# Moving two VectorE steps and one ScalarE step ahead of a weight split in a mixture-of-experts loop

## The chip, the cores and the metric

One core of a Trainium2 chip runs the whole layer as one program. The metric is the device time of one execution in microseconds; lower is better. Engines run their own instruction lists in order and wait for each other on semaphores: TensorE (PE) multiplies, ScalarE (ACT) and VectorE (DVE) do elementwise work, GpSimd (POOL) issues gathers and scatters, SyncE (SP) issues the loads of weights.

## The reference

A hybrid encoder layer over 1536 tokens of 1024 channels: two mixers (a gated spatial one and windowed attention), then a hierarchical mixture of experts. Only the last part matters here:

```python
def expert_block(args):
    xblk, e = args
    hid = jax.nn.silu(xblk @ w_gate[e]) * (xblk @ w_up[e])
    return hid @ w_down[e]

yb = lax.map(expert_block, (xb, block_e)).reshape(P, D)
y = jnp.zeros((T + 1, D), h.dtype).at[slot_tok].add(yb * slot_w[:, None])
```

Each token goes to two of 32 experts. The token rows of an expert are padded to blocks of 128. `w_gate` and `w_up` of an expert are 1024x512, `w_down` is 512x1024, all float32.

## The kernel before, in words

The mixers and the routing take the first two thirds of the time; then the expert loop runs over the blocks, one block of 128 rows in each trip, from trip 1 (written out once) through a hardware loop from 2 to `m`, with a short prologue and an epilogue.

**Split products.** Each float32 product is made of three matmuls over rounded parts: hi by hi, hi by lo and lo by hi. ScalarE makes the hi part by a rounding copy, and VectorE makes the lo part, the raw value less hi. This holds for the weights (`split_hi`, `split_lo`, in halves 0 and 1 of 128x2048 numbers, for g = gate, u = up, d = down), for the turned input rows (`x_hi`, `x_lo`, L2071 and L2142, two pieces each) and for the turned hidden rows (`hidden_hi`, `hidden_lo`, L2086 and L2157).

**TensorE in trip i** (`tensor`): `gate_up(i)` (gate product of block i into one PSUM bank, then its up product into another, 48 matmuls), `turn_x(i + 1)` (eight transposes of the gathered rows of the next block, L1984), `down(i - 1)` (24 matmuls), `turn_hidden(i)` (four transposes of `hid`, L2018). The first matmul of `gate_up` is on L1994, the first of `down` on L2008. `turn_hidden(i)` waits for `hid` of block i; `gate_up(i + 1)` waits for `x_lo(i + 1)` and, half by half, for the lo weights; `down(i)` waits for `hidden_lo(i)`. In trip 1 the order differs: `down(0)` lies between the gate and the up product, so that `turn_x(2)` is followed at once by `turn_hidden(1)`. The epilogue runs `gate_up(m + 1, "g")`, `down(m)`, `gate_up(m + 1, "u")`.

**ScalarE in body(i)** does, in order: g half 0 of the next block, `tanh(i)` (L2076), g half 1, u half 0, `x_hi(i + 1)`, u half 1, d half 0, `weigh(i - 1)` (scales the result rows, L2082), d half 1, `hidden_hi(i)`. **VectorE in body(i)**: g half 0, `glu_gate(i)` (L2148), g half 1, u half 0, `glu_up(i)` (L2153, which writes `hid`), `x_lo(i + 1)`, u half 1, d half 0, d half 1, `hidden_lo(i)`. A split of weights of half h waits until the data has landed and until TensorE has used the old half (`used`), and `split_lo` waits for its `split_hi`. `glu_up(i)` waits for `used["u"]` of both halves, the end of the up product.

**Loads.** Each weight has one raw buffer (`held_wg`, `held_wu`, `held_wd`), in two halves of 1 MB. The SyncE list issues the load of the block after next (of the next block for d) in the order g0, g1, u0, u1, d0, d1, each once VectorE has finished the split of that half (`lo_done`). A load is left out where the block has the same expert as the one before. GpSimd gathers the rows of block i + 2 after `turn_x(i + 1)` has read the buffer, and scatters block i - 1 after `weigh(i - 1)`; the next `weigh` waits until that scatter has landed (a copy into `e_prv` on POOL comes in between).

Of the kernel before, what the change touches and what calls it, by code (L numbers as in the profile page):

```python
# [1892 lines left out]
def experts(nc, a, held):  # L1893
# [34 lines left out]
    def half(t, h):  # L1928

        k = t.shape[1] // 2  # L1930
        return t[:, h * k:(h + 1) * k, :]

    def first(i):
        return isinstance(i, int) and i == 0


    def blocks(eng):

        eng.wait_ge(tab_in, 2 * 16)
        return eng.value_load(tab[0:1, 2 * TW + 2:2 * TW + 3], min_val=2 * T // P - 3, max_val=MAXB - 3)  # L1940
# [115 lines left out]
    def scalar(act):  # L2056
        def split_hi(i, w, h):

            act.wait_ge(w_in[w][h], (i + 2) * 16)
            if not first(i):  # L2060
                act.wait_ge(used[w], i * 2 + (h - 1))
            elif w == "g":
                act.wait_ge(s_up_ps, 1)
            else:
                act.wait_ge(s_up_ps if w == "u" else s_down_ps, 2)
            act.activation(half(hi[w], h), half(raw[w], h), ACT.Copy).then_inc(hi_done[w], 1)  # L2066

        def x_hi(i):
            for b in range(2):
                act.wait_ge(x_ps, i * 2 + (b + 5))  # L2070
                act.activation(half(xT_hi, b), ps_x[b][:].rearrange("p (k q) -> p k q", k=4),  # L2071
                               ACT.Copy).then_inc(x_hi_done, 1)

        def tanh(i):
            act.wait_ge(used["g"], i * 2 + 2)
            act.activation(th, ps_g[:], ACT.Tanh, scale=0.5).then_inc(tanh_done, 1)  # L2076

        def weigh(i):
            act.wait_ge(used["d"], i * 2 + 2)
            act.wait_ge(shifted, i + 1)  # L2080
            for h in range(2):
                act.activation(yo[:, h * 512:(h + 1) * 512], ps_y[h][:], ACT.Copy, scale=prv[:, 1:2]).then_inc(yo_done, 1)  # L2082

        def hidden_hi(i):
            act.wait_ge(h_ps, i + 3)
            act.activation(hidT_hi, ps_h[:].rearrange("p (k q) -> p k q", k=DE // P), ACT.Copy).then_inc(hid_hi_done, 1)  # L2086

        def body(i):
            split_hi(i + 1, "g", 0)
            tanh(i)  # L2090
            split_hi(i + 1, "g", 1)
            split_hi(i + 1, "u", 0)
            x_hi(i + 1)
            split_hi(i + 1, "u", 1)
            split_hi(i, "d", 0)
            weigh(i - 1)
            split_hi(i, "d", 1)
            hidden_hi(i)

        chosen_act = held["chosen_act"]  # L2100
        split_hi(0, "g", 0)
        split_hi(0, "g", 1)
        chosen_act["tanh"](act, 1)
        chosen_act["turned_hidden"](act, 0)
        split_hi(0, "u", 0)
        split_hi(0, "u", 1)
        chosen_act["turned_hidden"](act, 1)
        chosen_act["weigh"](act, 0)
        x_hi(0)
        split_hi(0, "d", 0)  # L2110
        split_hi(1, "g", 0)
        chosen_act["weigh"](act, 1)
        tanh(0)
        split_hi(1, "g", 1)
        split_hi(0, "d", 1)
        x_hi(1)
        hidden_hi(0)
        split_hi(1, "u", 0)
        split_hi(1, "u", 1)
        body(1)  # L2120
        m = blocks(act)
        with act.Fori(2, m + 1) as i:
            body(i)
        tanh(m + 1)
        split_hi(m + 1, "d", 0)
        split_hi(m + 1, "d", 1)
        weigh(m)
        hidden_hi(m + 1)
        weigh(m + 1)

    def vector(dve):
        dve.sem_inc(lo_done["d"], 2)

        def split_lo(i, w, h):

            dve.wait_ge(hi_done[w], i * 2 + (h + 1))
            dve.tensor_tensor(half(lo[w], h), half(raw[w], h), half(hi[w], h).bitcast(F32), ALU.subtract).then_inc(lo_done[w], 1)  # L2137

        def x_lo(i):
            for b in range(2):  # L2140
                dve.wait_ge(x_hi_done, i * 2 + (b + 5))
                dve.tensor_tensor(half(xT_lo, b), ps_x[b][:].rearrange("p (k q) -> p k q", k=4),  # L2142
                                  half(xT_hi, b).bitcast(F32), ALU.subtract).then_inc(x_lo_done, 1)

        def glu_gate(i):

            dve.wait_ge(tanh_done, i + 3)
            dve.scalar_tensor_tensor(out=th, in0=th, scalar=1.0, in1=ps_g[:], op0=ALU.add, op1=ALU.mult).then_inc(glu_done, 1)  # L2148

        def glu_up(i):  # L2150
            dve.wait_ge(glu_done, i + 3)
            dve.wait_ge(used["u"], i * 2 + 2)
            dve.scalar_tensor_tensor(out=hid, in0=th, scalar=0.5, in1=ps_u[:], op0=ALU.mult, op1=ALU.mult).then_inc(hid_done, 1)  # L2153

        def hidden_lo(i):
            dve.wait_ge(hid_hi_done, i + 3)
            dve.tensor_tensor(hidT_lo, ps_h[:].rearrange("p (k q) -> p k q", k=DE // P), hidT_hi.bitcast(F32),  # L2157
                              ALU.subtract).then_inc(hid_lo_done, 1)

        def body(i):  # L2160
            split_lo(i + 1, "g", 0)
            glu_gate(i)
            split_lo(i + 1, "g", 1)
            split_lo(i + 1, "u", 0)
            glu_up(i)
            x_lo(i + 1)
            split_lo(i + 1, "u", 1)
            split_lo(i, "d", 0)
            split_lo(i, "d", 1)
            hidden_lo(i)  # L2170

        split_lo(0, "g", 0)
        split_lo(0, "g", 1)
        held["chosen_dve"]["glu"](dve, 1)
        split_lo(0, "u", 0)
        split_lo(0, "u", 1)
        x_lo(0)
        split_lo(0, "d", 0)
        split_lo(1, "g", 0)
        glu_gate(0)  # L2180
        split_lo(1, "g", 1)
        glu_up(0)
        x_lo(1)
        split_lo(0, "d", 1)
        hidden_lo(0)
        split_lo(1, "u", 0)
        split_lo(1, "u", 1)
        body(1)
        m = blocks(dve)
        with dve.Fori(2, m + 1) as i:  # L2190
            body(i)
        glu_gate(m + 1)
        split_lo(m + 1, "d", 0)
        split_lo(m + 1, "d", 1)
        glu_up(m + 1)
        hidden_lo(m + 1)
# [194 lines left out]
```

## Time and profile before

| What | us |
|---|---|
| median of three executions | 2113.71 (2113.36 to 2115.78) |
| the profiled execution, its time | 2113.9 |
| the profiled execution, its span | 2112.1 |
| PE busy / DVE busy / ACT busy | 2086.8 / 1278.4 / 1072.8 |
| granted clock of TensorE, mean | 0.997 of full speed |

The span is the time between the first and the last instruction that the trace has; the execution's own time is 1.8 us longer. PE is marked busy nearly all the time, but that average says little of single waits: they are read from the list of waits and from the timeline. A "window" row gives, for a stretch of time, the busy time of each engine in it and the mean busy share of the 16 DMA engines (a share can come out a little over 1).

### The profile page before, as it was taken

The numbers are of one execution on the slowest core, as the hardware profiler recorded it, in microseconds if no ns is written. First come the engines' busy times: TensorE is split into PE (matmuls) and PEld (weight loads), VectorE is DVE, ScalarE is ACT, GpSimd is POOL, SyncE is SP. The second block draws the span as 40 slices with busy tenths as digits, with TensorE's granted clock in tenths as the row PEclk, the third lists the DMA queues.
The fourth block names the chain that finished last, engine by engine and source line by source line (L and its number), as shares of the span: only waits on it lengthen the run. The fifth ranks groups of instructions, "written<-read, shape, count | busy, mean of one in ns | idle before, by whom it ended". The sixth has DMA issues, their size and how long they took to land.

```text
span 2112.1 us, 30313 instructions
## 1 busy us (share of the span) xinstructions
PE 2086.8 (99%) x10284; PEld 1733.2 (82%) x10284; DVE 1278.4 (61%) x1651; ACT 1072.8 (51%) x1584; POOL 467.8 (22%) x653
## 2 busy tenths in 40 slices
PE   8999999999999999999999999999999999999997
PEld 7788888888788888897888888757888888888886
DVE  5664233465554233565553424369999999998995
ACT  4553333344542432345533332138888888887884
POOL 4251011210451011203510012002222222122321
PEclk9999999999999999999999999999999999999999
DMA  7312322443113322552123224487998689999892
GB/s 226 101 41 90 97 84 92 137 181 99 62 52 114 100 90 80 174 170 75 41 80 95 86 80 168 176 347 276 362 383 319 235 313 335 384 376 370 289 343 64
DMA packets 108658, 379.46 MB, mean 180 GB/s; under 512 B 13506, under 2 KB 19827, under 8 KB 82964
## 3 DMA queue, kind: packets, MB, share of 16 engines
q1 hardware_dynamic: 91812, 335.64, 43.9%
q0 software_dynamic: 16752, 42.56, 7.5%
q8 instruction: 59, 0.97, 0.2%
q14 instruction: 35, 0.29, 0.0%
HBM read 402.78 MB, written 34.60 MB: 207 GB/s over the span
## 4 chain that ended last, share of the span: by engine, by line
PE 50%; DMA 4%; DVE 1%; ACT 1%; issue 1%; POOL 0%; POOLq 0%; SPq 0%; ACTq 0%; DVEq 0%
PE main L532 3%; PE main L534 3%; PE main L533 3%; DMA held_wu<-w_up_e 3%; PE main L2008 3%; PE main L2010 3%; PE main L2009 3%; PE main L1996 3%; PE aux L1994 3%; PE main L1994 3%; PE main L1995 3%; PE aux L1996 3%; PE aux L1995 3%; PE main L520 2%; PE main L522 2%; PE main L521 2%
## 5 line engine op out<-in xcount | busy, mean ns | idle before, releaser
L984 DVE TENSOR_TENSOR w_lo<-raw,w_hi 128x1024 fp32r<-128x1024 f32 (+1 forms) x216 | 250.4, 1180 | 316.7 <-ACT w_hi L728 316.6
L728 ACT ACTIVATE w_hi<-raw 128x1024 fp32r<-128x1024 f32 (+1 forms) x216 | 211.5, 1005 | 143.4 <-PE main L534 73.9
L532 PE MATMUL main<-e_g_hi,w_hi 128*128 128x512 f32 x576 | 237.4, 412 | 0.0
L534 PE MATMUL main<-e_g_hi,w_lo 128*128 128x512 f32 x576 | 225.7, 392 | 0.0
L533 PE MATMUL main<-e_g_lo,w_hi 128*128 128x512 f32 x576 | 225.0, 391 | 0.0
L2137 DVE TENSOR_TENSOR e_d_lo<-held_wd,e_d_hi 128x2048 fp32r<-128x2048 f32 x76 | 173.8, 2289 | 52.1 <-ACT e_d_hi L2066 51.9
L520 PE MATMUL main<-w_hi,e_g_hi 128*128 128x512 f32 (+1 forms) x560 | 203.7, 364 | 1.2 <-DVE e_g_lo L998 0.6
L522 PE MATMUL main<-w_hi,e_g_lo 128*128 128x512 f32 (+1 forms) x560 | 200.1, 357 | 0.0
L521 PE MATMUL main<-w_lo,e_g_hi 128*128 128x512 f32 (+1 forms) x560 | 199.9, 357 | 0.0
L2137 DVE TENSOR_TENSOR e_u_lo<-held_wu,e_u_hi 128x2048 fp32r<-128x2048 f32 x76 | 173.4, 2284 | 14.0 <-ACT e_u_hi L2066 14.0
L2137 DVE TENSOR_TENSOR e_g_lo<-held_wg,e_g_hi 128x2048 fp32r<-128x2048 f32 x76 | 173.6, 2284 | 3.7 <-ACT e_g_hi L2066 3.7
L2066 ACT ACTIVATE e_u_hi<-held_wu 128x2048 fp32r<-128x2048 f32 x76 | 145.7, 1920 | 31.2 <-PE main L1996 15.9
L2066 ACT ACTIVATE e_d_hi<-held_wd 128x2048 fp32r<-128x2048 f32 x76 | 145.8, 1918 | 21.4 <-PE main L2010 11.5
L2066 ACT ACTIVATE e_g_hi<-held_wg 128x2048 fp32r<-128x2048 f32 x76 | 145.9, 1919 | 14.8 <-DMA held_wg<-w_gate_e 13.8
L534 PEld LDWEIGHTS main<-e_g_hi,w_lo 128*128 128x128 f32 x576 | 108.4, 188 | 23.3
L533 PEld LDWEIGHTS main<-e_g_lo,w_hi 128*128 128x128 f32 x576 | 109.1, 189 | 19.1
L532 PEld LDWEIGHTS main<-e_g_hi,w_hi 128*128 128x128 f32 x576 | 109.0, 189 | 18.8
L1994 PE MATMUL aux<-e_g_hi,e_xT_hi 128*128 128x512 f32 x304 | 122.2, 402 | 0.6 <-DVE e_xT_lo L2142 0.5
L2008 PE MATMUL main<-e_d_hi,e_hidT_hi 128*128 128x512 f32 x304 | 121.6, 400 | 0.7 <-DVE e_hidT_lo L2157 0.7
L819 ACT ACTIVATE pr<-sm,stat,rsq 128x384 f32<-128x384 f32 (+1 forms) x96 | 64.5, 671 | 111.7 <-DVE stat L1251 105.7
L520 PEld LDWEIGHTS main<-w_hi,e_g_hi 128*128 128x128 f32 x560 | 106.5, 190 | 16.2 <-DVE e_g_lo L998 1.0
L522 PEld LDWEIGHTS main<-w_hi,e_g_lo 128*128 128x128 f32 x560 | 106.4, 190 | 15.2
(360 smaller groups left out, 4704.4 us busy)
## 6 DMA issues: line engine op xcount, KB each, us to landing
held_wg<-w_gate_e SPq DMA_DIRECT2D x78, 1024.0 KB
held_wu<-w_up_e SPq DMA_DIRECT2D x78, 1024.0 KB
held_wd<-w_down_e SPq DMA_DIRECT2D x76, 1024.0 KB
raw<-w_in SPq DMA_DIRECT2D x120, 512.0 KB, 3.6
raw<-w_proj_b SPq DMA_DIRECT2D x24, 512.0 KB, 3.6
raw<-w_proj_a SPq DMA_DIRECT2D x24, 512.0 KB, 3.7
raw<-w_out SPq DMA_DIRECT2D x24, 512.0 KB, 4.1
raw<-w_in SPq DMA_DIRECT2D x24, 256.0 KB, 4.5
```

Source lines behind the costliest of these rows:

```text
L520: pe.matmul(bank[:, 0:n], stat_hi(k), hi[:, k, 0:n], start=(k == 0), stop=False)
L521: pe.matmul(bank[:, 0:n], stat_hi(k), lo[:, k, 0:n], start=False, stop=False)
L522: mm = pe.matmul(bank[:, 0:n], stat_lo(k), hi[:, k, 0:n], start=False, stop=(k == KT - 1))
L532: pe.matmul(bank[:], hi[:, k, :], mov_hi[:, k, :], start=(k == 0), stop=False)
L533: pe.matmul(bank[:], hi[:, k, :], mov_lo[:, k, :], start=False, stop=False)
L534: mm = pe.matmul(bank[:], lo[:, k, :], mov_hi[:, k, :], start=False, stop=(k == KT - 1))
L728: act.activation(hi, buf, ACT.Copy).then_inc(w_hi_done, 1)
L984: dve.tensor_tensor(lo, buf, hi.bitcast(F32), ALU.subtract).then_inc(w_split, 1)
L1994: pe.matmul(ps[:], xT_hi[:, k, :], hi[w][:, k, :], start=(k == 0), stop=False)
L2008: pe.matmul(ps_y[h][:], hidT_hi[:, k, :], hi["d"][:, k, c], start=(k == 0), stop=False)
L2066: act.activation(half(hi[w], h), half(raw[w], h), ACT.Copy).then_inc(hi_done[w], 1)
L2137: dve.tensor_tensor(half(lo[w], h), half(raw[w], h), half(hi[w], h).bitcast(F32), ALU.subtract).then_inc(lo_done[w], 1)
```

## The change

In ScalarE's body, `x_hi(i + 1)` now comes before the split of u half 0 and no longer after it. In VectorE's body, `glu_up(i)` and `x_lo(i + 1)` come before the split of u half 0 and no longer after it. Nothing is added or taken away; the prologue, the epilogue and the lists of the other engines are the same.

```diff
@@ scalar, body(i)
             split_hi(i + 1, "g", 1)
+            x_hi(i + 1)
             split_hi(i + 1, "u", 0)
-            x_hi(i + 1)
             split_hi(i + 1, "u", 1)
@@ vector, body(i)
             split_lo(i + 1, "g", 1)
-            split_lo(i + 1, "u", 0)
             glu_up(i)
             x_lo(i + 1)
+            split_lo(i + 1, "u", 0)
             split_lo(i + 1, "u", 1)
```

## Rows read from the trace of the kernel before

**Rows 1.** The page: span and number of instructions

```profile
span 2112.1 us, 30313 instructions
```

**Rows 2.** Waits of PE, expert loop (who for whom: us, times, longest)

```profile
PE aux L2018 <- DVE e_hid L2153: 2.6, 4, 1.4
...
PE aux L1994 <- DVE e_xT_lo L2142: 0.5, 1, 0.5
```

**Rows 3.** One of 35 windows of one block's length each

```profile
1843.37:1861.13 17.76, 17.76 (x87) 14.90 (x86) 16.29 (x12) 14.50 (x12) 3.42 (x4) 1.00 1.01 391
```

**Rows 4.** Timeline, trip 1 (start, length, engine, line, tiles, idle before)

```profile
1448.69 2.29 DVE L2137 TENSOR_TENSOR e_u_lo<-held_wu,e_u_hi 128x2048 fp32r<-128x2048 f32 x1 [3.19 <-ACT e_u_hi L2066]
...
1448.97 0.40 PE L1996 MATMUL main<-e_u_hi,e_xT_lo 128*128 128x512 f32 x1
...
1449.85 1.08 ACT L2071 ACTIVATE e_xT_hi<-aux 128x512 fp32r<-128x512 f32 x2 [1.20 <-PE aux L1984]
...
1450.89 0.68 DVE L2153 SCALAR_TENSOR_TENSOR e_hid<-e_th,main 128x512 f32<-128x512 f32 x1
...
1451.63 0.75 PE L2018 MATMUL aux<-ident,e_hid 128*128 128x128 f32 x4 [1.37 <-DVE e_hid L2153]
...
1452.91 0.47 PE L1994 MATMUL aux<-e_g_hi,e_xT_hi 128*128 128x512 f32 x1 [0.53 <-DVE e_xT_lo L2142]
```

**Rows 5.** The chain that ended last, prologue (start, length, what)

```profile
1431.37 0.61 ACT e_xT_hi L2071
1432.00 0.70 DVE e_xT_lo L2142
```

**Rows 6.** Timelines of ACT and DVE, one block in the middle

```profile
1727.82 1.92 ACT L2066 ACTIVATE e_u_hi<-held_wu 128x2048 fp32r<-128x2048 f32 x1 [0.38 <-PE main L1996]
1730.93 1.09 ACT L2071 ACTIVATE e_xT_hi<-aux 128x512 fp32r<-128x512 f32 x2 [1.19 <-PE aux L1984]
1731.90 1.92 ACT L2066 ACTIVATE e_u_hi<-held_wu 128x2048 fp32r<-128x2048 f32 x1
...
1730.00 2.28 DVE L2137 TENSOR_TENSOR e_u_lo<-held_wu,e_u_hi 128x2048 fp32r<-128x2048 f32 x1
1732.20 0.68 DVE L2153 SCALAR_TENSOR_TENSOR e_hid<-e_th,main 128x512 f32<-128x512 f32 x1
```

**Rows 7.** Timeline of SP's queue, the same block (issues of two halves each)

```profile
1727.63 2.90 SPq L1890 DMA_DIRECT2D held_wg<-w_gate_e  x2
1732.63 4.08 SPq L1890 DMA_DIRECT2D held_wu<-w_up_e  x2
```

**Rows 8.** Timelines of ACT and PE, end of a long stretch of loads

```profile
1945.88 1.92 ACT L2066 ACTIVATE e_u_hi<-held_wu 128x2048 fp32r<-128x2048 f32 x1 [2.71 <-DMA held_wu<-w_up_e]
...
1960.37 1.92 ACT L2066 ACTIVATE e_g_hi<-held_wg 128x2048 fp32r<-128x2048 f32 x1 [1.02 <-DMA held_wg<-w_gate_e]
1964.21 1.92 ACT L2066 ACTIVATE e_u_hi<-held_wu 128x2048 fp32r<-128x2048 f32 x1 [1.91 <-DMA held_wu<-w_up_e]
...
1932.01 0.64 PE L2018 MATMUL aux<-ident,e_hid 128*128 128x128 f32 x4
...
1950.77 0.75 PE L2018 MATMUL aux<-ident,e_hid 128*128 128x128 f32 x4 [0.84 <-DVE e_hid L2153]
...
1969.10 0.75 PE L2018 MATMUL aux<-ident,e_hid 128*128 128x128 f32 x4 [0.17 <-DVE e_hid L2153]
```

**Rows 9.** Timelines of ACT, DVE and PE, last trip and epilogue

```profile
2070.19 1.09 ACT L2071 ACTIVATE e_xT_hi<-aux 128x512 fp32r<-128x512 f32 x2 [1.19 <-PE aux L1984]
...
2081.42 0.68 DVE L2157 TENSOR_TENSOR e_hidT_lo<-aux,e_hidT_hi 128x512 fp32r<-128x512 f32 x1
...
2082.34 0.49 PE L2008 MATMUL main<-e_d_hi,e_hidT_hi 128*128 128x512 f32 x1 [0.32 <-DVE e_hidT_lo L2157]
```

**Rows 10.** Timeline of POOL, one block in the middle

```profile
1712.37 2.20 POOL L2232 COPY e_prv<-held_slots 128x2 f32 x1 [7.27 <-DMA y<-e_yo,e_prv]
...
1714.52 0.17 POOL L2205 COPY e_nxt<-held_slots 128x2 f32 x1
```

## The prediction, made before the changed kernel was run

> **What bounds the kernel now.** I read the page first, for the span of 2112.1 us [rows 1], then the expert loop, where the diff lies, in windows of one block each. A window of 17.76 us has PE busy for all 17.76, DVE for 16.29 and ACT for 14.50 [rows 3]; so do nearly all of the 35. PE sets the pace of the loop, and an order of the splits can give time only where PE waits for DVE or ACT. The DMA share is the second thing to see there: 20 of the 35 windows stand at 0.99 or more, in runs of 6, 2, 10 and 2 blocks. In those the loads take all the bandwidth there is, and a block's loads take longer than PE's 17.76 us: u half 0 landed 18.33 us apart (1945.88 and 1964.21) [rows 8]. PE stays ahead only by the slack that the raw buffers hold.
>
> Third, the list of PE's waits, from the start of the loop to the end of the program: four waits for `hid`, 2.6 us in all with 1.4 the longest, and one of 0.5 for `x_lo` [rows 2]. That is nearly all that the change can take away. The timeline says where they are. In trip 1, `glu_up(1)` could have run from the end of the up product at 1449.37 (1448.97 + 0.40), but DVE was in the split of u0 from 1448.69 and it started at 1450.89; PE's transposes of `hid` came at 1451.63 and the next gate product at 1452.91 [rows 4]. Two more are at the end of the run of ten saturated blocks. From 1932.01 PE's transposes of `hid` came at 1950.77 and 1969.10, which is 18.76 and 18.33 and not 17.76 apart, so 1.00 and 0.57 us lost [rows 8]. There DVE and ACT wait for u0 to land, with `glu_up` queued behind. The fourth is in the epilogue, which stays as it is.
>
> **Part 1: trip 1.** The moved steps keep their durations. `x_hi` starts at 1449.85, since its transposes release it [rows 4], not the split before it; on DVE `glu_up` starts at about 1449.4, takes 0.68 and ends near 1450.1, before PE is through with its transposes. PE then waits only for the first piece of `x_lo`. DVE starts that 0.63 us after ACT started on its piece, and takes 0.70 [rows 5]; PE follows 0.05 behind, as it does after `hid` (1450.89 + 0.68 to 1451.63, 0.06) [rows 4]. So the gate product starts at 1449.85 + 0.63 + 0.70 + 0.05 = 1451.23 and not at 1452.91: **1.68 us gained**. Bounds: nothing, if some other input of PE is late, and 2.2, if PE had no wait at all there. I take 1.68; it rests on measured steps.
>
> What is late next: u0's hi starts 0.97 after `x_hi` (1730.93 to 1731.90), its lo 1.92 + 0.03 later, then DVE's splits start 2.20 apart (1730.00 to 1732.20) [rows 6]. Lo of u0 ends at 1449.85 + 0.97 + 1.95 + 2.28 = 1455.05; PE asks for it after 24 of 72 matmuls, a third of a period without its transposes, so about 5.5 us after 1451.23: 1456.7. It is covered by 1.6 us. `hidden_lo(1)` starts 2.92 + 4 x 2.20 = 11.72 after `x_hi` and ends 1462.3; `down(1)` asks at about 1463.0. If these covers went, the 1.68 would shrink by the shortfall.
>
> **Part 2: a block in the middle.** ACT did u0 from 1727.82 and then waited 1.19 us for `x_hi`'s transposes, at 1730.93. Now it stands idle until 1730.93 and u0 starts at 1731.90 [rows 6], 4.08 later. DVE starts u0's lo at 1731.90 + 1.95 = 1733.85 and not at 1730.00: 3.85 later; by then it has done `glu_up` and `x_lo` (0.68 and twice 0.70), which come earlier by about 1.7 and 1.2. Through u1, d0, d1 the delay melts, for DVE used to stand idle 1.47 us of a block (17.76 less 16.29 [rows 3]), all of it ahead of d1: u1 and d0 are 2.1 later, d1, `hidden_lo` and the next g0 0.5 later. DVE's work stays 16.3 of 17.76 us, so the delay doesn't grow from trip to trip. The nearest asker, `down`, wants `hidden_lo` over 5 us after it is done. Here the move costs **0**, hidden behind PE's matmuls; what it costs without that cover is the 3.85.
>
> **Part 3: the loads.** No load is moved on SP, but each waits for its lo split, so u0's is issued 3.85 later (1732.63 becomes 1736.5) and d0 behind it 2.1; g0 goes from 1727.63 to 1728.1 [rows 7]. A half takes 18.33 / 6 = 3.06 us when the loads are saturated [rows 8]. At the start of a saturated run, the queue holds g0 and g1 only, 6.1 us of work, and u0 comes 8.4 us behind: the DMA engines stand still for up to 2.3 us once, and by the u0 issue the whole run is late by at most 1736.5 - 2 x 3.06 - 1727.63 = 2.7 us. Afterwards six halves fill 18.3 us of a 17.76 us block, so the queue isn't dry again. Bounds: 0 (loads were queued already) and 2.7; I take 2.7.
>
> **Part 4: the end of the long run.** Now `hid` stands behind g1's split, not u0's. g1's hi began on its landing at 1960.37, 3.84 us before u0's [rows 8]. With all 2.7 us of lag: 1963.07, lo at 1965.02, `glu_up` 1967.22, `hid` with PE at 1967.96, against an unstalled 1932.01 + 2 x 17.76 = 1967.53. The first piece of `x_lo`, 0.60 behind `glu_up` and 0.75 long with its hand-over, is ready at 1968.57, 0.5 after PE wants it. So 0.5 us of the 1.57 stays: **1.07 gained**, bounds 0 and 1.57. u0, landed at 1966.9, has its lo by 1971.4, before PE's up product at 1973.5.
>
> **Part 5: the epilogue.** `down(m)` comes early there, behind one gate product. `hidden_lo(m)` started 11.23 after `x_hi` (2070.19 to 2081.42) and PE was already waiting for it: it began `down` at 2082.34 [rows 9]. By the new order it starts 11.72 after `x_hi`: **0.5 us lost**, between 0 and 0.6.
>
> **Sum**: -1.68 - 1.07 + 0.5 = -2.25 us. The profiled execution took 2113.9, its span 2112.1 [rows 1] and 1.8 around it; the span should become 2109.9, and that execution's time 2111.65. The median of the runs was 0.2 lower, so 2111.4.
>
> **GpSimd** shares the change too. A copy of two numbers into `e_prv` took 2.20 us while DVE was in a split, the same kind of copy 0.17 right after it [rows 10]. DVE now has its four splits u0, u1, d0, d1 in one piece around the time of the scatter, which can hold the scatter back by about one split, 2.2 us. The next scaling of rows waits for that scatter, and POOL's gather stands behind it in line; the next scaling comes after PE's `down`, whose end the transposes of `hid` mark at 1932.01 - 12 x 17.76 = 1718.89 [rows 8], and the copy ended at 1714.57, so there are over 4 us. So it costs nothing in the sum, and 2.2 us at most a block where that cover is gone. The Trainium skill, SBUF — State Buffer, "SBUF: two separate sides", says that a VectorE instruction with two SBUF inputs holds a port pair that GpSimd shares, so the other blocks for the whole instruction; by that rule the price is one split for each operation of GpSimd that meets one, and the sum stays at -2.25 as long as the 4 us hold. The trace agrees: that 2.20 us copy ended with the split.
>
> **The rivals.** (a) *Nothing arrives.* The wait in trip 1 turns into one for another input, such as the rest of `x_lo`, and the lag of the loads eats all of part 4. Only the epilogue's 0.5 is left: 2114.2. For it: DVE has 1.5 us to spare in a block. Against it: each hand-over in part 1 is measured. (b) *The loads run dry again and again*, which is the slower side. If the 2.3 us of standstill of part 3 came in every block of the run of ten and not once, PE would end it some 20 us later: about 2132. It decides from the point where six halves take less than PE's 17.76 us, or where the queue empties before u0's issue; with 3.06 us a half it keeps 0.6 us more work each block than PE takes, and the share near 1.0 in all ten windows speaks against it. (c) *More is gained than the profiled execution shows.* The three executions differ by 2.4 us, and such a difference can come from the saturated runs; one that lost 4 us there could win them all. 2109. (d) The scatter of the GpSimd rule comes too late in all 36 trips of the loop: 2113.7 + 36 x 0.3 = 2124 if it overran by 0.3 us a block.
>
> **How the numbers follow.** Forecast -2.25 us: 0.76. (a) 0.11, (b) 0.05, (c) 0.06, (d) 0.02. A measurement of this kernel tells a difference of 0.2% from none, which is 4.2 us: under 2109.5 is faster, over 2117.9 slower. The likeliest case and (a) are both inside; so faster 0.06, within 0.2% 0.87, slower 0.07. The likeliest case with its bounds (gain of 1.68 + 1.57 without loss; only part 1 less the epilogue) runs from 2110.5 to 2112.5. With the scatter of three executions and (a), I give 2109.8 to 2115.0.
>
> **What would show it.** In the list of PE's waits, the 1.4 us for `hid` in trip 1 is gone and the gate product of trip 2 begins some 1.4 us after the first transposes of x are out. In a block in the middle, ACT is idle some 3.6 us ahead of `x_hi`, and u0's lo starts 2.9 us after `x_hi`. The period stays 17.76. SP's u loads come 3.85 later, the DMA share stays about 1.0 in the same windows, and PE loses at most 0.5 us at the end of the run of ten. `down` in the epilogue starts 0.5 us later in relation to the last `x_hi`. The prediction is wrong if the period of an ordinary block grows, if u0 or u1 become what PE waits for, or if the loads lag by clearly more than 2.7 us.

## The result and the profile after

The change made the kernel slower: 2143.18 us, median of four executions (2137.20 to 2147.26), against 2113.53 (2113.24 to 2115.78) for the kernel before, a ratio of 1.0131 with a 95% interval of 1.0117 to 1.0145. The ratio is the estimate on record with its interval; the two medians by themselves give 1.0140. I had forecast 2111.4 and nothing measurable. The profiled execution has a span of 2135.4 us, 23.3 more than before [rows 1]; at 2137.20 it was the quickest of the four, so its rows show the loss at its smallest.

First, the list of PE's waits in the expert loop and behind it, of the changed kernel:

```profile
PE aux L1984 <- DMA e_xg<-h2s,e_nxt: 24.8, 19, 2.1
PE main L2008 <- DVE e_hidT_lo L2157: 1.2, 2, 0.8
PE aux L2018 <- DVE e_hid L2153: 1.1, 2, 0.9
PE aux L1994 <- DVE e_xT_lo L2142: 0.4, 1, 0.4
```

The four waits for `hid` of 2.6 us in [rows 2] have become two of 1.1. A new line stands above them: nineteen times the transposes of the next block's rows waited until the gathered rows `e_xg` had landed. Nothing of that kind was in the kernel before. The 24.8 us are the loss of this execution, and a little of it was won back.

Next, what was meant to happen. The timeline of trip 1 of the changed kernel, TensorE, VectorE and ScalarE:

```profile
1445.34 0.40 PE L1996 MATMUL main<-e_u_hi,e_xT_lo 128*128 128x512 f32 x1
...
1446.59 0.75 PE L2018 MATMUL aux<-ident,e_hid 128*128 128x128 f32 x4
1447.77 0.47 PE L1994 MATMUL aux<-e_g_hi,e_xT_hi 128*128 128x512 f32 x1 [0.43 <-DVE e_xT_lo L2142]
...
1445.84 0.69 DVE L2153 SCALAR_TENSOR_TENSOR e_hid<-e_th,main 128x512 f32<-128x512 f32 x1 [3.99 <-PE main L1996]
1446.84 1.29 DVE L2142 TENSOR_TENSOR e_xT_lo<-aux,e_xT_hi 128x512 fp32r<-128x512 f32 x2 [0.31 <-ACT e_xT_hi L2071]
...
1446.21 1.09 ACT L2071 ACTIVATE e_xT_hi<-aux 128x512 fp32r<-128x512 f32 x2 [8.30 <-PE aux L1984]
```

From the end of the up product to the next gate product PE needs 2.03 us (1445.74 to 1447.77), where it needed 3.54 before [rows 4]. Part 1 was right: 1.51 us against the 1.68 forecast.

The middle of the loop, VectorE and SP's queue in a trip before the long run of loads, still of the changed kernel:

```profile
1788.66 0.68 DVE L2153 SCALAR_TENSOR_TENSOR e_hid<-e_th,main 128x512 f32<-128x512 f32 x1
1789.71 1.29 DVE L2142 TENSOR_TENSOR e_xT_lo<-aux,e_xT_hi 128x512 fp32r<-128x512 f32 x2 [0.38 <-ACT e_xT_hi L2071]
1792.01 4.49 DVE L2137 TENSOR_TENSOR e_u_lo<-held_wu,e_u_hi 128x2048 fp32r<-128x2048 f32 x2 [1.00 <-ACT e_u_hi L2066]
1796.42 4.49 DVE L2137 TENSOR_TENSOR e_d_lo<-held_wd,e_d_hi 128x2048 fp32r<-128x2048 f32 x2
...
1786.29 3.15 SPq L1890 DMA_DIRECT2D held_wg<-w_gate_e  x2
1794.64 2.55 SPq L1890 DMA_DIRECT2D held_wu<-w_up_e  x2
```

VectorE has the schedule of part 2: a pause of 1.00 us ahead of u0, then u0, u1, d0, d1 without a gap, 8.9 us long (the x2 rows are two splits each). The up load follows the gate load by 8.35 us, as worked out (8.4), where it was 5.0 before [rows 7].

Now the engine that I had costed at nothing. GpSimd's timeline, one turn in the long run of loads, of the changed kernel:

```profile
1870.64 1.00 POOL L2232 COPY e_prv<-held_slots 128x2 f32 x1 [10.62 <-DMA y<-e_yo,e_prv]
1871.59 2.26 POOL L2205 COPY e_nxt<-held_slots 128x2 f32 x1
1874.72 2.21 POOL L2208 DMA_INDIRECT e_xg<-h2s,e_nxt  x1 [0.87 <-ACT e_yo L2082]
1877.24 2.44 POOL L2212 DMA_INDIRECT y<-e_yo,e_prv  x1 [0.31 <-issue]
1889.99 0.76 POOL L2232 COPY e_prv<-held_slots 128x2 f32 x1 [10.32 <-DMA y<-e_yo,e_prv]
```

and one turn of the kernel before, in its run of ten saturated blocks:

```profile
1856.01 0.64 POOL L2232 COPY e_prv<-held_slots 128x2 f32 x1 [8.82 <-DMA y<-e_yo,e_prv]
1856.59 0.18 POOL L2205 COPY e_nxt<-held_slots 128x2 f32 x1
1857.64 1.05 POOL L2208 DMA_INDIRECT e_xg<-h2s,e_nxt  x1 [0.87 <-POOL e_nxt L2205]
1863.34 1.59 POOL L2212 DMA_INDIRECT y<-e_yo,e_prv  x1 [4.65 <-ACT e_yo L2082]
1874.04 0.37 POOL L2232 COPY e_prv<-held_slots 128x2 f32 x1 [9.10 <-DMA y<-e_yo,e_prv]
```

GpSimd's list is a ring: a scatter must land before `e_prv` is copied, then comes `e_nxt`, the next gather, and the next scatter. From start to start the hops are:

| hop, us | before | after |
|---|---|---|
| copy of `e_prv` to copy of `e_nxt` | 0.58 | 0.95 |
| copy of `e_nxt` to gather | 1.05 | 3.13 |
| gather to scatter, less the wait for `e_yo` | 5.70 - 4.65 = 1.05 | 2.52 |
| scatter, its landing, to copy of `e_prv` | 10.70 | 12.75 |
| the ring without that wait | 13.38 | 19.35 |

Some 0.3 us of the third hop after the change is idle time at issue that the wait covered before. VectorE in the same turn of the changed kernel:

```profile
1869.31 4.49 DVE L2137 TENSOR_TENSOR e_u_lo<-held_wu,e_u_hi 128x2048 fp32r<-128x2048 f32 x2 [1.00 <-ACT e_u_hi L2066]
1873.72 4.49 DVE L2137 TENSOR_TENSOR e_d_lo<-held_wd,e_d_hi 128x2048 fp32r<-128x2048 f32 x2
```

All four of GpSimd's operations start inside these splits. The copy of `e_prv` ends at 1871.64 and that of `e_nxt` at 1873.85, with the first and the second split (1871.60 and 1873.80); the gather and the scatter end at 1876.93 and 1879.68, which is not the end of a split.

Before, the ring had 4.65 us to spare. After, it has nothing to spare and is longer than PE's 17.76 us. The gather stands in this ring, so the whole loop turns at the ring's pace: in the nineteen blocks with a wait, PE's transposes of `hid` are 18.95 to 20.12 us apart. The windows of two blocks of the changed kernel, against [rows 3]:

```profile
1852.47:1872.11 19.64, 18.03 (x85) 14.82 (x84) 16.37 (x12) 14.13 (x13) 7.85 (x5) 1.00 0.99 355
1872.11:1891.22 19.11, 18.03 (x85) 14.82 (x84) 16.39 (x12) 14.14 (x13) 7.62 (x5) 1.00 1.00 363
```

PE is busy 18.03 of 19.64 and of 19.11 us, at the same granted clock of 1.00, and POOL is busy 7.85 and 7.62 us a block where it was 3.42. That last number points to the cause: GpSimd has the same work to do and is busy for more than twice as long.

### The profile page after: what moved, and what is told of

The parts are those of the page before. It is cut to its first block, busy times and chain, and to the rows that moved or that the text cites. A ratio compares the mean times of both kernels' runs of the same rounds, so it can differ in the third digit from the quotient of the medians.

```text
span 2135.4 us, 30313 instructions
## 1 busy us (share of the span) xinstructions
PE 2087.1 (98%) x10284; PEld 1728.6 (81%) x10284; DVE 1279.6 (60%) x1651; ACT 1060.7 (50%) x1584; POOL 571.6 (27%) x653
## 4 chain that ended last, share of the span: by engine, by line
PE 69%; DMA 16%; issue 6%; POOL 3%; ACT 2%; DVE 2%; POOLq 0%; ACTq 0%; DVEq 0%
DMA y<-e_yo,e_prv 11%; PE main L534 10%; PE main L532 10%; PE main L533 10%; PE main L520 6%; PE main L522 6%; PE main L521 6%; PE aux L566 2%; DMA e_xg<-h2s,e_nxt 2%; POOL e_nxt L2205 2%; PE aux L585 1%; PE main L585 1%; PE main L2008 1%; PE main L2010 1%; PE main L2009 1%
## 5 line engine op out<-in xcount | busy, mean ns | idle before, releaser
L2066 ACT ACTIVATE e_u_hi<-held_wu 128x2048 fp32r<-128x2048 f32 x76 | 141.4, 1917 | 0.0
L533 PEld LDWEIGHTS main<-e_g_lo,w_hi 128*128 128x128 f32 x576 | 109.1, 189 | 19.1
L2232 POOL COPY e_prv<-held_slots 128x2 f32 x36 | 35.7, 991 | 325.5 <-DMA y<-e_yo,e_prv 322.4
L2010 PE MATMUL main<-e_d_hi,e_hidT_lo 128*128 128x512 f32 x304 | 118.8, 391 | 0.0
```

What stands on the lines that cost most here:

```text
L533: pe.matmul(bank[:], hi[:, k, :], mov_lo[:, k, :], start=False, stop=False)
L2010: mm = pe.matmul(ps_y[h][:], hidT_lo[:, k, :], hi["d"][:, k, c], start=False, stop=(k == DE // P - 1))
```

## Experiments

The case before the first runs: theory A, the ring on GpSimd sets the pace; theory B, the later loads leave the DMA engines idle (rival b of the prediction, whose 2132 was the nearest of my numbers to the result). B came near the size, but had not the wait that the trace shows. The code below is shortened.

### GpSimd's gather ahead of the landing

```diff
@@ gpsimd, loop of the changed kernel
+            pool.wait_ge(x_ps, i * 2 + 8)
+            pool.wait_ge(x_in, i * 16 + 64)
+            gather(i + 2, i + 3)
             pool.wait_ge(y_out, i * 16 + 16)
             pool.tensor_copy(prv, entry(i - 1)).then_inc(shifted, 1)
-            pool.wait_ge(x_ps, i * 2 + 8)
-            pool.wait_ge(x_in, i * 16 + 64)
-            gather(i + 2, i + 3)
```

> The changed kernel, with one more move, on GpSimd alone: in each trip the gather of the rows of block i + 2 goes ahead of the wait for the landed scatter and of the copy into e_prv. Theory A (GpSimd's ring: scatter, landing, copy, copy, gather, scatter takes some 19.3 us against a period of 17.76, and the gathered rows come too late for the transposes): the gather no longer stands behind the landing, PE's wait for e_xg (24.8 us in 19 waits) goes, and the time falls to 2111 to 2114. Theory B (the later loads leave the DMA engines idle; rival b of the prediction): nothing about the loads is changed, so the time stays near 2140, and PE waits for the lo weights or hid once the rows are there.

Measured: 2118.49 us, 1.0014 of before (1.0003 to 1.0026). The waits for `e_xg` are gone, and most of the loss with them. PE's waits in that kernel:

```profile
PE main L2008 <- DVE e_hidT_lo L2157: 9.5, 10, 3.3
PE aux L1994 <- DVE e_xT_lo L2142: 0.6, 2, 0.4
PE aux L2018 <- DVE e_hid L2153: 0.2, 1, 0.2
```

The rule by which the loads are issued was not touched, which speaks against B. It does not yet rule B out: in the long run of loads the up load follows the gate load by 6.8 us in this kernel, where the changed one has over 9. And 9.5 us of waits ahead of `down` are new (the profiled execution was the slowest of the ten, at 2124.01), and the time is above my 2111 to 2114. Some cost came with this edit or stayed from the change.

### Each engine's part alone

```diff
@@ vector, body (run: VectorE alone)
-            split_lo(i + 1, "u", 0)
             glu_up(i)
             x_lo(i + 1)
+            split_lo(i + 1, "u", 0)
@@ scalar, body (run: ScalarE alone)
+            x_hi(i + 1)
             split_hi(i + 1, "u", 0)
-            x_hi(i + 1)
@@ vector, body (run: glu_up alone)
+            glu_up(i)
             split_lo(i + 1, "u", 0)
-            glu_up(i)
             x_lo(i + 1)
```

> The kernel before with VectorE's part of the change alone: glu_up and x_lo ahead of the split of u half 0, ScalarE in the old order. Theory A: the four splits u0, u1, d0, d1 of VectorE follow each other without a break, as in the changed kernel, so GpSimd's copies, gathers and scatters run into them and the time is slow too, 2125 to 2145, with PE waiting for e_xg. Theory B: the u loads are issued 2.8 us later and not 3.85, so less is lost: 2114 to 2128, and PE's waits are for weights.

Measured: 2131.73 us, 1.0070 (1.0047 to 1.0094). PE waited 16.8 us in 17 waits for `e_xg`. VectorE's half alone brings the wait on the gathered rows, as A says. The time is inside A's range of 2125 to 2145 and above B's of 2114 to 2128, and the kind of wait is A's.

> The kernel before with ScalarE's part of the change alone: x_hi ahead of the split of u half 0, VectorE in the old order. By the schedule of the rows, VectorE does u0's lo at x_hi + 2.92, glu_up at + 5.12, x_lo at + 5.72, and PE can start the gate product at + 6.47; with 11.65 us from there to the next x_hi the period is some 18.1 us, so 36 trips lose 0.36 us each: 2125 to 2128, PE waiting for hid and x_lo. Theory A expects no wait for e_xg here, since x_lo still parts the splits of u0 and u1. Theory B, with the same late u loads as in the changed kernel, expects at least the changed kernel's loss in the saturated windows: 2140 or more.

Measured: 2138.16 us, 1.0105 (1.0082 to 1.0128), and not one wait for `e_xg`. The line that speaks is PE's weight loads, in small waits at 37 of the 38 blocks:

```profile
PEld aux L2018 <- DVE e_hid L2153: 24.7, 37, 5.6
```

The period is 18.13 us in most blocks, as worked out (18.1). The 0.37 us above 17.76 make 13 us over 36 trips. I had left out trips 1 and 2 and the epilogue, which lost 3.8, 2.2 and 3.8 us more. The time is far above the 2125 to 2128 that I gave, and close to B's 2140; but the loss is not where B has it. The up loads follow the gate loads by 6.9 us, against 5.0 before, and yet the blocks of the long run take the same 18.13 us as the others, up to the last five. So ScalarE's half by itself is slow for another reason: `hid` now waits for a split that starts after `x_hi`. In the full change VectorE's half takes that away, so this loss is not part of the 29 us.

> The kernel before with glu_up alone moved ahead of the split of u half 0 on VectorE; x_lo stays behind it, ScalarE in the old order. VectorE keeps its breaks: x_lo between u0 and u1, and some idle time ahead of d1. Theory A: no wait for e_xg, and the waits for hid are gone: 2111 to 2114. Theory B: u loads only 0.7 us later, so also near 2113; this run does not part A from B, it asks whether the wanted gain is to be had this way.

Measured: 2116.57 us, 1.0010 (0.9998 to 1.0021), PE never waiting for `e_xg`. The wait for `hid` in trip 1 went (17.98 us for that block), but trip 2 took 21.85 us, waiting for `x_lo`. The end of the long run waits for `x_lo` too (2.8 us in four waits). The time is above my 2111 to 2114, and it is not a way to the gain.

### One SBUF input in place of two

This parts the ring's length from its reason. In the hardware loop VectorE's splits of weights stay in place and in number, but subtract a fixed bank of PSUM in place of the hi part. The lo parts are then not the rounding rest, so this kernel and the two below do not compute the layer; only their times are used.

```diff
@@ vector, split_lo, inside the hardware loop
-            dve.tensor_tensor(half(lo[w], h), half(raw[w], h), half(hi[w], h).bitcast(F32), ALU.subtract)
+            other = main[3][:].unsqueeze(1).to_broadcast([P, 4, 512])
+            dve.tensor_tensor(to, frm, other, ALU.subtract)    # to, frm: the same halves, as [P, 4, 512]
```

> The changed kernel; in the hardware loop the splits of weights on VectorE subtract a fixed bank of PSUM (one number per column, repeated) from the raw half in place of the hi half. So each has one input in SBUF and not two, at the same shape; order, waits, loads and what TensorE does stay. The lo weights are not the rounding rest any more, and the outputs of most blocks are not the reference's. Theory A1 (GpSimd's operations are held up by VectorE instructions with two SBUF inputs): the copy into e_nxt takes some 0.18 us and not 2.26, the scatter is issued 0.8 us sooner and lands within about 10 us, the ring on GpSimd falls under 17.76, the waits for e_xg go, and the time falls to 2111 to 2119. Theory A2 (GpSimd waits for VectorE whatever its operands): nothing changes, 2137 to 2147. Theory B (loads): nothing changes either.

Measured: 2112.13 us, 0.9990 (0.9981 to 1.0000). All 29 us are gone, at an unchanged duration of the split. GpSimd in the long run of loads of this kernel:

```profile
1872.40 0.18 POOL L2238 COPY e_prv<-held_slots 128x2 f32 x1 [9.04 <-DMA y<-e_yo,e_prv]
1872.76 0.18 POOL L2211 COPY e_nxt<-held_slots 128x2 f32 x1 [0.17 <-issue]
1874.18 1.06 POOL L2214 DMA_INDIRECT e_xg<-h2s,e_nxt  x1 [1.24 <-issue]
1880.38 1.60 POOL L2218 DMA_INDIRECT y<-e_yo,e_prv  x1 [5.14 <-issue]
1891.03 0.18 POOL L2238 COPY e_prv<-held_slots 128x2 f32 x1 [9.05 <-DMA y<-e_yo,e_prv]
```

The copies take 0.18, the gather 1.06, the scatter 1.60 and lands in time; the ring has 5.14 us to spare again. This run also rules B out: the up load still follows the gate load by 8.37 us in the first four blocks of the long run, as the changed order makes it, and the blocks there take 17.76 us up to its last three. And the VectorE rows say that the split itself is what it was (min, median, max of 66 in ns):

```profile
L2143 DVE TENSOR_TENSOR e_u_lo<-held_wu,main x66: 2277/2286/2292, 1500.3 to 2071.4; 128x2048 fp32r<-128x2048 f32 x66
```

> The same replacement in the kernel before, as the control: what the replacement does by itself. In the hardware loop the lo weights are not the rounding rest, so most outputs are not the reference's. The duration of a split should stay near 2.29 us. All theories expect 2112 to 2116; under A1 the copies into e_prv lose their 2.2 us cases as well.

Measured: 2114.42 us, 0.9996 (0.9986 to 1.0005). By itself the replacement gives nothing, so the 2112.13 is the change's own effect with GpSimd left free.

```diff
@@ vector, split_lo (run: up weights alone)
-            if not isinstance(i, int):
+            if not isinstance(i, int) and w == "u":
```

> The changed kernel, with the one-SBUF-input form for the two splits of up weights alone; those of gate and down weights keep two. The lo parts of the up weights are not the rounding rest in the hardware loop, so most outputs are not the reference's. It halves the cover of VectorE's two-input work behind x_lo. Theory A1: the copies that met the u splits (e_nxt at 2.26 us) fall to 0.2 in most trips, the scatter behind d0 and d1 keeps its 2.4; the ring comes to about 17, near the period: 2111 to 2122. If only the full block of four splits matters, or none, it is 2137 or 2112.

Measured: 2113.80 us, 0.9992 (0.9983 to 1.0002). Half of the cover is enough: `e_nxt` takes 0.18 us again, and `e_xg` is waited for once, 1.2 us, near the start of the loop. The scatters still take 2.35 us in the median of the hardware loop, 2.5 in the first two blocks of the long run and 1.74 in most of the others, but a longer scatter alone doesn't bring the ring to the period: 3.1 us or more are spare in every turn of that run.

### The ring with one hop less

```diff
@@ gpsimd, loop of the changed kernel
-            gather(i + 2, i + 3)                  # copies e_nxt, then gathers
+            gather(i + 2, i + 3, copy=False)
             pool.wait_ge(shifted, i)
             pool.wait_ge(yo_done, i * 2 + 4)
             scatter()
+            pool.wait_ge(x_in, i * 16 + 80)
+            copy_next(i + 3)
```

> The changed kernel; GpSimd copies the entry of the next gather into e_nxt already behind the scatter of the trip before, once the gather in flight has landed, and no longer between the landed scatter and the gather. Every value is the same. Theory A1 (ring on GpSimd, lengthened by VectorE's splits): the ring of the changed kernel, some 19.3 us, loses the copy of 2.26 us and its hand-over of up to 0.9; at 16.2 to 17.0 it is under the period of 17.76, the waits for e_xg shrink to few or none, and the time falls to 2111 to 2119. If the ring were not what sets the pace, it stays at 2137 to 2147.

Measured: 2118.20 us, 1.0012 (1.0003 to 1.0022). With two-input splits and the full new order, taking one copy out of the ring gives back 25 us, since the rest of it fits into the period: with hardly anything to spare in the first three blocks of the long run (0.3 us ahead of the scatter), and with about 4 us in most of the later ones. `e_xg` is waited for twice, 2.7 us.

> The same early copy in the kernel before, as the control. There the ring takes some 13.5 us of the 17.76 and GpSimd then waits over 4 us for the scaled rows, so an earlier gather changes nothing: 2112 to 2116. If an earlier gather costs bandwidth where the loads are saturated, as the early gather of 2121.9 may say, 2116 to 2120.

Measured: 2116.93 us, 1.0000 (0.9990 to 1.0010). In the kernel before, the place of that copy makes no measurable difference. The median is 0.9 us above the 2112 to 2116 of my first case and inside the second; the ratio doesn't support the second.

### What the early gather costs

```diff
@@ gpsimd, loop of the kernel before: as in the first experiment, ScalarE and VectorE in the old order
```

> The kernel before with GpSimd's gather ahead of the wait for the landed scatter, as in the run that showed 2118.5, and the old order on ScalarE and VectorE. It parts what is left of that run's loss. If the later loads make it, this kernel stands at the time of before, 2113 to 2116. If the early gather takes bandwidth or holds the scatter back, it is slower too, 2116 to 2120.

Measured: 2121.88 us, 1.0028 (1.0012 to 1.0045), above both of my ranges. So the early gather costs by itself, and the 1.0014 of the first experiment needs no late loads to explain it. Its profile shows both a longer stall at the end of the long run (blocks of 18.8 to 19.1 us) and a `down` in the epilogue that waits for its weights (3.9 us).

The second is to be read from the trace. With the gather first, the copy into `e_prv` stands behind it, and so behind PE's `turn_x`; ScalarE's `weigh` waits for that copy, and d half 1 stands behind `weigh` in ScalarE's list. Two lists of waits, ScalarE in this kernel and in the first experiment; the kernel before has no such wait:

```profile
ACT e_yo L2082 <- POOL e_prv L2237: 38.7, 16, 4.0
ACT e_yo L2082 <- POOL e_prv L2237: 35.1, 10, 5.5
```

and the chain ahead of the `down` in the epilogue of this kernel:

```profile
2079.29 4.28 POOL e_prv L2237
...
2084.24 0.68 ACT e_yo L2082
2084.92 1.81 ACT e_d_hi L2066
2086.76 0.55 DVE e_d_lo L2137
...
2088.97 0.69 DVE e_hidT_lo L2157
...
2089.88 0.49 PE main L2008
```

The last interval between transposes of `hid` is 23.28 us here and was 18.44. The stall at the end of the long run is another: there ScalarE waits for the up weights to land, which come 19.0 to 19.2 us apart. Why the gather's place does that is not settled.

### The new order in trip 1 alone

```diff
@@ vector, body (on scalar, x_hi in the same way)
+            if isinstance(i, int):      # trip 1, written out: the new order
+                glu_up(i); x_lo(i + 1); split_lo(i + 1, "u", 0)
+            else:                       # the hardware loop: the old one
```

> The new order in trip 1 alone, on both engines; the hardware loop keeps the old one. Trip 1 is where 1.7 us of PE's waits lie, and in the changed kernel it did take 17.99 us and not 19.73. Under both theories the loop then behaves as before: a gain of 1.7 us, 0.08%. If trip 2 or the loads behind it give the gain back, the difference is within 0.5 us of nothing.

Measured: 2116.00 us, 1.0008 (0.9998 to 1.0017): no gain. Trip 1 took 17.99 us instead of 19.73, but the three blocks after it 19.90, 19.37 and 19.64 instead of 18.62 and twice 17.76, with two waits for `e_xg` among them (2.7 us). None of the versions that compute the layer beat the kernel before.

## Why the prediction was wrong, step by step

**Where PE waits** was right: trip 1 and the end of the run of ten blocks hold what the order can win.

**Part 1** was right: 1.51 us for 1.68. **Part 2** had VectorE's new schedule to a tenth of a microsecond, and its own claim holds: the four splits in a row delay nobody on PE or ACT, as the run with one SBUF input shows. **Part 3** had the issue times, 8.35 us from gate to up load, and the loads' lag did not turn into a loss beyond part 4's: with GpSimd left free the same rule of issue goes with 2112.13. Its price of a half rests on one distance of 18.33 us; the two before it were 18.17 and 19.51. **Part 4** can be checked only in that kernel: the blocks there took 17.81, 18.18 and 17.84 us, 0.55 lost for a forecast of 0.5. The kernel before lost 1.82 in its three blocks there; the forecast had counted two of them, 1.57. **Part 5**: the last interval between transposes of `hid` is 18.95 in the changed kernel and was 18.44, so 0.51 lost for 0.5. The sum of the five parts, -2.25 us, is about what the changed order did once VectorE's splits had one SBUF input: 2112.13 against 2114.25 for the kernel before over the same runs, -2.1 us, at the edge of what these runs can tell.

**The step that failed** is the paragraph on GpSimd, which put a term of some 25 to 30 us at nothing: "So it costs nothing in the sum, and 2.2 us at most a block where that cover is gone." Three things in it were wrong.

- It counted one operation that meets a split, the scatter. But the splits became one piece of 8.9 us, and GpSimd goes through its two copies, gather and scatter in a row, each longer than before. The first three hops of the table are 0.4, 2.1 and 1.5 us longer.
- It left the landing out. From the issue of the scatter to its landing the median grew from 10.4 to 12.5 us in the long run of loads. The experiment with one SBUF input has 10.3 over the loop. The fourth hop is 2.0 us longer by it, so the ring 6.0 in all.
- It took the next `weigh` as the one who asks, over 4 us away. The gather stands in the same ring, and a ring has no slack against a deadline, only against the period: 13.4 + 6.0 = 19.4 against 17.76.

The row for it was in hand: the 2.20 us copy of [rows 10] against 0.17. So was the ring, in GpSimd's timeline, with 4.65 us to spare. Rival (d) had the mechanism, but I gave it 2 in 100 and 0.3 us a block, without adding up the ring. The wait for the 128x2 copy is also what the Trainium skill, SBUF — State Buffer, "SBUF: two separate sides", would have it be: it says that a VectorE instruction with two SBUF inputs locks a GpSimd operation that reads SBUF out of a shared port pair for as long as it runs. The runs here agree for the copy: same duration, same order, one SBUF input, and `e_nxt` falls from 2.26 to 0.18 us. The prediction cited that rule, and applied it to one operation only.

**Why only 19 of the blocks.** The ring was too long where the loads were saturated as well. Where they were not, the changed kernel kept 17.76 us: a scatter issued at 1638.70 let the copy start at 1646.55, 7.85 us later and not 12.75. Block by block the two kernels can be laid side by side: of the nineteen long blocks fifteen are among the 20 that have a DMA share of 0.99 or more in the kernel before, and the other four come directly before or behind such a run. So it seems that two things make the loss together, VectorE's unbroken splits and full DMA engines. The experiments varied the first alone; that full DMA engines are needed too is read from where the blocks lie, and not shown by a run.

**What stays open**: why the up weights land later at the end of the long run with the early gather, and the 2.4 us by which the kernel with the early copy stands above before, where -2.25 was on offer. Its trace says only where they are: 2.1 us in the third block, with a wait for `e_xg` of 1.8, and about 1 us each at the end of the long run and in the last interval.

## What to carry to other kernels

When steps are reordered on one engine, list the rings of the engines that share something with it, and add each ring up hop by hop against the period; slack to the next deadline isn't slack in a ring. Look at where the pauses of VectorE's two-input work lie as at a resource: a gap or an instruction that reads PSUM lets GpSimd through, and closing the gaps can cost more than they did. An operation that is short in one row and long in another of the same profile has told its price already; multiply it by all operations that will meet the same cause.

## What the runs showed of the hardware

- A GpSimd copy of 128x2 numbers takes 0.18 us by itself and 2.26 us behind a 128x2048 `tensor_tensor` of VectorE with both inputs in SBUF. With one of the inputs in PSUM and the same 2.29 us on VectorE it takes 0.18 us in all 33 copies into `e_nxt` from 1500 us on.
- Indirect DMAs issued by GpSimd take longer then too: the gather 2.2 us for 1.05, the scatter 2.44 for 1.60, and the scatter lands 12.5 us after its issue for 10.4. With one input in PSUM they are back at 1.06, 1.60 and 10.4 in the long run of loads.
